# First attention of a two-layer kernel: split values stationary, probabilities moving in 256 columns

## What is computed

```
q = rmsnorm(zq, q_norm_g); k = rmsnorm(zk, k_norm_g); v = zv
y_a = dilated_attention(q, k, v)
y = concat([rmsnorm(y_c, g_out_conv), rmsnorm(y_a, g_out_attn)])
x = x + y @ w_out
```

## Time and profile before

| | us |
|---|---|
| median of three runs | 2596.24 (2596.04 to 2597.03) |
| the profiled execution's own time | 2594.65 |
| its span, first to last instruction | 2593.0 |
| PE busy in the span | 2542.1 (98%) |
| DVE, ACT, POOL busy | 1296.6, 1043.0, 1265.1 |
| mean granted TensorE clock | 0.995 of full speed |

### The profile page before, as it was taken

The page is one execution under the profiler, slowest core; times in us unless marked ns, Lnnn a source line. Parts: engine busy times, 40 slices in busy tenths (PEclk is TensorE's granted clock), DMA queues, the critical chain, the costliest instruction groups (busy, mean ns, idle before and its releaser), DMA issues.

```text
span 2593.0 us, 35106 instructions
## 1 busy us (share of the span) xinstructions
PE 2542.1 (98%) x12506; PEld 2121.9 (82%) x12506; DVE 1296.6 (50%) x2500; ACT 1043.0 (40%) x1955; POOL 1265.1 (49%) x940
## 2 busy tenths in 40 slices
PE   7999999999999999999999999989999999999999
PEld 6888888887888888888877777779888888888887
DVE  5314446178666663225367888677237333333222
ACT  6345553253333332214256666486234333232120
POOL 2122224457666665444525554364256666656441
PEclk9999999999999999999999999999999999999999
DMA  4242312412222235220323122220322222226311
GB/s 156 73 118 90 95 54 76 159 58 98 82 90 82 90 130 203 82 65 16 110 77 98 59 68 70 95 82 21 147 82 73 82 75 89 82 99 225 111 47 71
DMA packets 90205, 238.47 MB, mean 92 GB/s; under 512 B 10256, under 2 KB 23856, under 8 KB 89776
## 3 DMA queue, kind: packets, MB, share of 16 engines
q1 hardware_dynamic: 90032, 236.21, 26.8%
HBM read 180.60 MB, written 51.38 MB: 89 GB/s over the span
## 4 chain that ended last, share of the span: by engine, by line
PE 68%; DVE 3%; ACT 2%; issue 1%; POOL 1%; DMA 1%; SPq 0%; ACTq 0%; DVEq 0%; POOLq 0%
PE PS L943 9%; PE PS L944 9%; PE PS L945 9%; PE PS L961 6%; PE PS L963 6%; PE PS L962 6%; PE PS L690 5%; PE PS L692 4%; PE PS L691 4%; PE PS L1213 2%; PE PS L1193 1%; DVE YT L2086 1%; PE PS L913 1%; PE PS L1178 1%; PE PS L1179 1%
## 5 line engine op out<-in xcount | busy, mean ns | idle before, releaser
L690 PE MATMUL PS<-Hh,Wl 128*128 128x512 f32 x1072 | 438.3, 409 | 12.3 <-DVE Hl L1344 9.7
L692 PE MATMUL PS<-Hh,Wh 128*128 128x512 f32 x1072 | 421.0, 393 | 0.0
L691 PE MATMUL PS<-Hl,Wh 128*128 128x512 f32 x1072 | 419.8, 392 | 0.0
L3135 POOL TENSOR_TENSOR Wl<-Wr,Wh 128x512 fp32r<-128x512 f32 (+1 forms) x158 | 210.1, 1352 | 341.6 <-ACT Wh L2270 341.4
L3239 POOL TENSOR_TENSOR RG<-RW,RG 128x512 fp32r<-128x512 f32 x176 | 246.4, 1404 | 134.0 <-ACT RG L2546 133.8
L1757 DVE TENSOR_TENSOR XA<-PS,XA 128x512 f32<-128x512 f32 x192 | 132.5, 691 | 331.4 <-PE PS L963 331.4
L961 PE MATMUL PS<-Hh,RG 128*128 128x512 f32 x704 | 274.1, 389 | 0.5 <-issue 0.4
L963 PE MATMUL PS<-Hh,RG 128*128 128x512 f32 x704 | 273.9, 389 | 0.0
L962 PE MATMUL PS<-Hl,RG 128*128 128x512 f32 x704 | 273.9, 389 | 0.0
L3239 POOL TENSOR_TENSOR RG<-SW,RG 128x512 fp32r<-128x512 f32 x120 | 164.7, 1373 | 175.3 <-ACT RG L2546 150.0
L943 PE MATMUL PS<-Hh,RG 128*128 128x512 f32 x640 | 249.0, 389 | 0.0
(11 more groups left out here) (356 smaller groups left out, 5136.1 us busy)
## 6 DMA issues: line engine op xcount, KB each, us to landing
RW<-in_wg SPq DMA_DIRECT2D x44, 512.0 KB, 3.6
RW<-in_wu SPq DMA_DIRECT2D x44, 512.0 KB, 4.5
R<-in_wd SPq DMA_DIRECT2D x88, 256.0 KB, 3.0
hgscr<-GB SPq DMA_DIRECT2D x44, 512.0 KB, 2.6
G<-hgscr SPq DMA_DIRECT2D x40, 512.0 KB, 6.8
Wr<-in_wi SPq DMA_DIRECT2D x27, 512.0 KB, 3.4
Wr<-in_wo SPq DMA_DIRECT2D x16, 512.0 KB, 3.4
spill<-X SPq DMA_DIRECT2D x16, 512.0 KB, 2.6
```

Source lines behind the costliest of these rows:

```text
L690: pe.matmul(ps(b), k.Wl[:, s, wc], xh[:, kx, sl], start=kk == 0, stop=False)
L691: pe.matmul(ps(b), k.Wh[:, s, wc], xl[:, kx, sl], start=False, stop=False)
L692: i = pe.matmul(ps(b), k.Wh[:, s, wc], xh[:, kx, sl], start=False, stop=kk == nk - 1)
L3135: i = pool.tensor_tensor(k.Wl[:, s, c], k.Wr[:, s, c], k.Wh[:, s, c].bitcast(F32), ALU.subtract)
```

## The change

Values: each of the 8 position blocks is evicted twice, by ACT as the f32r high part and by DVE as the low part (value minus high part), into staging buffers `VS`. SP sends them out: head 0 straight to its place `V2[0]` (64 KB per block, rows of 512 bytes), the other heads (448 KB per block, rows of 512 bytes) to a scratch tensor in HBM, and waits for all of these before its weave goes on. `V2[h % 2]` holds for one head and each key block 128 columns: 64 of the head's high parts, 64 of its low parts (swapped for odd heads); `values_load` fetches the next head in tick i = 2.

Output: `V2` is the stationary operand and the transposed probabilities move, in 256 columns: the high part of 128 queries, then the low part. Bank 3 then holds, by features, high x high, high x low and (in the other 64 partitions) low x high. ACT copies the last (`att_c`), DVE adds the first two (a reduction), POOL adds the copy four ticks after the step's own tick. `sums_row` spreads the reciprocals of four blocks over the rows by four transposes on PE (16 times in all), and DVE multiplies half a head by them.

Probabilities: ACT copies all n blocks of the transposed probabilities as their high part, DVE subtracts that from PSUM for the low part and only this frees banks 6 and 7.

Norm: the outputs already lie by features. `attention1_norm` squares four tiles of 128x1024 on ACT, DVE adds them up, PE sums over features in 8 one-column matmuls, ACT takes the root, PE spreads it in 8 transposes, DVE applies it with the gain. 32 transposes, 32 scalings and 32 squares of 128x128 go.

```
--- attention1, tensor
-                if i > 3 and k.wide(1, r) is not None:
-                    pe.wait_ge(*at("att_ptv", 1, k.wide(1, r)))
+                if i == 4 and h:
+                    pe.wait_ge(*at("y_own", h - 1, 1))
...
-                for c in range(i + 1):
-                    m = pe.matmul(ps(3, 128), k.PT[:, r % 2, 128 * c:128 * c + 128],
-                                  k.Vt[:, c, 128 * (h // 2):128 * (h // 2) + 128], start=c == 0, stop=c == i)
+                pe.wait_ge(*at("att_lo", 1, r))
+                for c in range(i + 1):
+                    m = pe.matmul(ps(3, 256), k.V2[h % 2][:, c, :], k.PT[r % 2][:, c, :], start=c == 0, stop=c == i)
                 m.then_inc(*up(("full", 3), "att_o", 1, r))
+            for h, half in k.row_due(s):
+                sums_row(h, half)
--- attention1, vector
-                if i > 3:
-                    w = 128 * (i + 1) - 512
-                    dve.wait_ge(*at("att_t", 1, r))
-                    dve.tensor_copy(k.PT[:, r % 2, 512:512 + w], ps(7, w)).then_inc(*up("att_ptv", "att_ptv", 1, r))
+                dve.wait_ge(*at("att_t", 1, r))
+                dve.wait_ge(*at("att_pt", 1, r))
+                dve.tensor_tensor(k.PT[r % 2][:, 0:i + 1, 128:256],
+                                  k.PS[:, 512 * 6:512 * 6 + W].rearrange("p (c n) -> p c n", c=i + 1),
+                                  k.PT[r % 2][:, 0:i + 1, 0:128].bitcast(F32), ALU.subtract).then_inc(
+                    *up(("free", 6), "att_lo", 1, r))
...
-                dve.tensor_scalar(out, k.PS[:, o:o + 64], k.rx[:, r:r + 1], None, ALU.mult).then_inc(
-                    *up(("free", 3), "att_y", 1, r))
+                dve.wait_ge(*at("att_c", 1, r))
+                dve.tensor_reduce(k.ya(h)[own, 128 * i:128 * i + 128],
+                                  k.PS[own, 512 * 3:512 * 3 + 256].rearrange("p (z q) -> p q z", z=2),
+                                  mybir.AxisListType.X, ALU.add).then_inc(*up(("free", 3), "att_y", 1, r))
+            for h, half in k.row_due(s, 1):
+                sums_row(h, half)
--- attention1, scalar
-                act.activation(PT[:, r % 2, 0:w], ps(6, w), ACT.Copy).then_inc(*up(("free", 6), "att_pt", a, r))
+                act.activation(k.PT[r % 2][:, 0:i + 1, 0:128],
+                               k.PS[:, 512 * 6:512 * 6 + W].rearrange("p (c n) -> p c n", c=i + 1), ACT.Copy).then_inc(
+                    *up("att_pt", "att_pt", 1, r))
+            if 3 <= s < n + 3:
+                r = s - 3
+                own, other = k.sides(ATT1[r][0])
+                act.wait_ge(*at("att_o", 1, r))
+                if r >= 2:
+                    act.wait_ge(*at("y_add", r - 2))
+                act.activation(k.sml[own, 256 + 128 * (r % 2):384 + 128 * (r % 2)], k.PS[other, 512 * 3:512 * 3 + 128],
+                               ACT.Copy).then_inc(*up("yn_a", "att_c", 1, r))
--- attention1, gpsimd
+            if s >= 4:
+                r = s - 4
...
+                pool.wait_ge(*at("att_c", 1, r))
+                pool.wait_ge(*at("att_y", 1, r))
...
+                pool.tensor_tensor(y, y, k.sml[own, 256 + 128 * (r % 2):384 + 128 * (r % 2)], ALU.add).then_inc(
+                    *up("rot_g", "y_add", r))
--- sync
+    for i in range(8):
+        v = k.VS[i][:, :, :, :].bitcast(F32).rearrange("p h z n -> p (h z n)")
+        sp.wait_ge(*at("vt", i))
+        sp.dma_start(k.V2[0][:, i, :].bitcast(F32), v[:, 0:128]).then_inc(*up(("d_s", i), "v2_in", 0, i))
+        sp.dma_start(k.vs.rearrange("h p n -> p h n")[:, 1:8, 128 * i:128 * i + 128],
+                     v[:, 128:1024].rearrange("p (h n) -> p h n", h=7)).then_inc(*up(("d_y", i), "v_kept", i))
+    for i in range(8):
+        sp.wait_ge(*at("v_kept", i))
     bg.add(tables1())
```

More of the change, by code:

```diff
@@ L484, in ya, with sides, row_due @@
         return k.YX[:, :] if h < 2 else k.QT[:, h // 2 - 1, :]
+    def sides(h):
+        own = slice(64 * (h % 2), 64 * (h % 2) + 64)
+        return own, slice(64 - 64 * (h % 2), 128 - 64 * (h % 2))
+    def row_due(s, late=0):
+        return [(h, half) for h in range(8) for half in range(2) if s == 8 * h + 10 + 2 * half + late]
+    k.sides, k.row_due = sides, row_due
     def eps_at(half):
@@ L781, in tensor, with sums_row @@
                 qk_slot(between[i])
+    def sums_row(h, half):
+        r = 8 * h + 4 * half
+        take(7)
+        pe.wait_ge(*at("att_rec", 1, r + 3))
+        for i in range(4):
+            m = pe.transpose(ps(7)[:, 128 * i:128 * i + 128], k.rx[:, r + i:r + i + 1].to_broadcast([128, 128]), ident)
+        m.then_inc(*up(("full", 7), "y_row", h, half))
     def attention1():
         n = len(ATT1)
-        for s in range(n + 3):
+        for s in range(n + 6):
             if 2 <= s <= n + 1:
@@ L1392, in vector, with sums_row @@
         qk_slot(t)
+    for i in range(8):
+        dve.wait_ge(*at("v", i))
+        dve.wait_ge(*at("vt_hi", i))
+        dve.scalar_tensor_tensor(out=k.VS[i][:, :, 1, :], in0=ps(i).rearrange("p (h n) -> p h n", h=8),
+                                 scalar=k.sml[:, 112 + i:113 + i], in1=k.VS[i][:, :, 0, :].bitcast(F32), op0=ALU.mult,
+                                 op1=ALU.subtract).then_inc(*up(("free", i), "vt", i))
+    def sums_row(h, half):
+        own, _ = k.sides(h)
+        y = k.ya(h)[own, half_of(half)]
+        dve.wait_ge(*at("y_row", h, half))
+        dve.wait_ge(*at("y_add", 8 * h + 3 + 4 * half))
+        dve.tensor_tensor(y, y, k.PS[own, 512 * 7:512 * 8], ALU.mult).then_inc(*up(("free", 7), "y_own", h, half))
     def attention1():
         n = len(ATT1)
-        for s in range(n + 3):
+        for s in range(n + 6):
             if 2 <= s <= n + 1:
@@ L1450, in attention1_turn @@
+        for c in range(1, 4):
+            dve.wait_ge(*at("y_sq", 0))
+            dve.wait_ge(*at("y_sq", c))
+            if c > 1:
+                dve.wait_ge(*at("y_sum", c - 1))
+            dve.tensor_tensor(k.PP[:, 2, :], k.PP[:, 2, :], k.PP[:, (c + 1) % 2, :], ALU.add).then_inc(*up("yn_v", "y_sum", c))
             yield
+        for _ in range(4):
             yield
+        dve.wait_ge(*at("y_std"))
+        dve.reciprocal(k.sml[:, 80:88], k.sml[:, 88:96]).then_inc(*up("yn_v", "y_root"))
@@ new lines, in attention1_norm @@
+        for _ in range(2):
+            yield
+        for half in range(2):
+            sl = half_of(half)
+            dve.wait_ge(*at("y_spread", half))
+            for c in range(4):
+                i = dve.scalar_tensor_tensor(out=k.KT[:, c, sl], in0=k.ya(2 * c)[:, sl], scalar=col("g_out_attn", c),
+                                             in1=ps(6 + half), op0=ALU.mult, op1=ALU.mult)
+                if c == 3:
+                    i.then_inc(*up(("free", 6 + half), "yk", half))
+                yield
@@ L3555, in tables1 @@
                 key_load(h + 1)
+            if i == 2 and h < 7:
+                sp.wait_ge(*at("att_o", 1, 8 * h - 1) if h else at("v_kept", 6))
+                values_load(h + 1)
             if i == 4 and h < 7:
```

202 lines of the change are left out of this document (113 added, 89 removed).

## The result

| | before | after |
|---|---|---|
| median of the runs | 2596.14 us (2595.13 to 2597.03) | **2637.02 us** (2634.62 to 2639.22) |
| profiled execution, its span | 2594.65, 2593.0 | 2636.77, 2635.5 |
| first to last exponential of the attention | 169.94 to 368.41 = 198.5 | 169.41 to 408.37 = **239.0** |

(PE is TensorE, PEld its weight loads, DVE VectorE, ACT ScalarE, POOL GpSimd, SP the engine that issues the loads and stores. Tile i stands for a head's step with i + 1 key blocks; "the interval 4 to 5" is the time from the start of the exponential of tile 4 to that of tile 5.)

The account below looks back on a forecast made before the run. The prediction took a closed ACT-DVE chain (copy, subtract, maximum, exponential) to bound the changed attention: +18.5 us there, +1 ahead, -2.5 behind, sum +17, so 2613 us. Range 2598 to 2636 us.

Parts of the forecast that it names:

- The sign: Whole kernel: the change makes it slower, chance 0.83, against 0.10 for the same and 0.07 for faster.
- One closed chain over two engines: Attention ticks: none can be shorter than copy + subtract + maximum + exp on ACT and DVE; attention 217 us against 198.5.
- Start, "+1, between 0 and 6": Ahead of the attention: storing values by 16 DMAs, with SP waiting for all, costs +1 us, between 0 and 6.
- The table of eight intervals: Attention: each tick's interval from chain, ACT extras and PE's round, together 26.4 us per head; PE alone would need 22.6.
- PE 1.07 ahead: Attention tick 2: PE runs 1.07 us ahead, so the interval is 2.36 us although PE's round is 3.43.
- DVE's 64-partition reduction and the 16 row products lie beside exp: nothing.: Attention: these added DVE operations run beside ACT's exponential and cost nothing.
- Query loads, 3 of 0 to 8: Attention: ACT's waits for query loads, 8.0 us before, add 3 us, anywhere from 0 to 8.
- PE -27 us: PE's own work: cheaper output matmuls, less added row transposes and with a shorter final part, make it fall by 27 us.
- Behind, -2.5: After the attention: the last three output groups and the shorter final part, less one row group, save 2.5 us.
- Rival 3: Attention: PE's idling lowers the granted clock; once per head adds 16 us, 2629 us; chance 0.07.
- Rival 4: Attention: loads drive the chain, ACT waits of 4 us in every head add 8 x 3, 2635 us; chance 0.05.
- Rival 1: Attention: PE still sets the pace and loses 27 us of work, 2569 us; chance 0.05.

Follow-up runs that it names:

- rows early: Changed kernel with the second row product of a head and the transposes before it one tick earlier, and the first product too: 2636.82 us, ratio 1.0146.
- the last one: Changed kernel plus all three edits of order and place, head 1's keys and queries fetched earlier, query split at tile 2, two-part bank hand-over: 2592.57 us, ratio 0.9983.

## Why the prediction failed

The sign, which had a chance of 0.83, and the mechanism were right: a closed chain over ACT and DVE made the attention longer though PE had less to do. The size was not: 41 us against 17, and 1 us outside the range. Of the 22 us by which the attention overran its forecast (239.0 against 217), the trace of the changed kernel gives 7.3 to the load of head 1's keys, which the sum did not have, some 5 to two ticks of the table (an estimate from heads 3 and 4, times seven) and at most some 4 to the wait for the row product (what the profile of rows early lost). The rest, 5 us or more, stays open. By the prediction's own steps:

- *"One closed chain over two engines" sets the tick.* Right: 57 and 60 of 64 waits; an added microsecond of subtraction costs about one; opened, the chain gives 29 us back. The durations were as worked out: copies of 1024 and 896 columns took 1.026 and 0.908 us (1.02 and 0.91 were drawn on from 512), the subtraction of 1024 took 1.22. The Trainium skill's estimate for the copy of 1024 columns (ScalarE: Activation LUTs, What ACT_TABLE_LOAD costs) was 1039 ns; the trace is 13 ns under it.
- *Start, "+1, between 0 and 6".* The step that failed most: 7.3 us (the interval 4 to 5 of head 0, 11.29, less the chain's 4.0), and inside the attention, not ahead of it. The first copies were looked at, and not the load of head 1's keys, which SP issues behind its wait for all the stores and which ACT's next copy stands behind. SP's queue was named in the text, its next customer was not. Issuing it earlier did not mend it by itself, since the DMA engines are full there.
- *The table of eight intervals.* Heads 3 and 4, in which ACT waits for no load, took 29.2 and 29.3 us, where the table has 26.4 and the forecast 27 to 28 with what was added. Ticks 0 and 1 came out (6.5 us from head 3 to head 4, against 6.63), in part by luck: the table has a query split in tick 1, but the program runs each split behind the exponential of its tick, so it lands one tick later, and in its place ACT stood 0.45 us for the eight transposes. The misplaced splits hardly move the sum. Ticks 2 and 3 failed: 4.71 in the table, 5.4 and 5.5 measured (intervals 1 to 2 and 2 to 3, and 0.2 since the table counts from end to end). *"PE 1.07 ahead"* was the term: PE needs the subtraction of eight blocks before it can send the next transpose, which starts only 0.3 us ahead of the exponential of tile 1 (266.42), its round then takes 3.55 us, and ACT's copy waits for its end:

```profile
266.10 0.33 PE L819 MATMUL PS<-mats,PP 128*128 128x128 f32 x1
...
269.65 0.38 PE L819 MATMUL PS<-mats,PP 128*128 128x128 f32 x2
```

```profile
270.07 0.39 ACT L2517 ACTIVATE PT<-PS 128x256 fp32r<-128x256 f32 x1 [0.61 <-PE PS L819]
```

- *"DVE's 64-partition reduction and the 16 row products lie beside exp: nothing."* The step failed as a wait: not their 0.69 us, but that PE's transposes of tile 4 wait for the second product of the head before (17.5 us, 7 times), and behind the longest of these waits run at the lower clock. The interval 5 to 6, where the chain with its query split gives 4.1, took 4.56 to 5.25 us in heads 1 to 7; in head 3 that is the weight split, which ACT had to take there too. With the wait removed the attention was 3.9 us shorter in one profile and the whole was not, so what it was worth stays open.
- *Query loads, 3 of 0 to 8.* One of 3.58 us made the interval 1 to 2 of head 5 6.01 us, where the others have 2.2 to 3.3: right in size.
- *PE -27 us.* It was 15 to 16, which cost nothing here but decides what the change could ever bring. Output matmuls are 0.12 us apart, as taken, but where PE runs without standing the 0.08 us behind each group stayed (five take 0.68 us, six 0.80, seven 0.92), and the spread rows cost 9.7, not 7.7.
- *Behind, -2.5.* From the last exponential to the end the profiles have 2224.6 us before, 2227.1 after and 2224.8 to 2233.8 in the variants. None shows the gain; the runs of one kernel spread over several microseconds, so how much was lost in its place isn't told apart.

Rival 3 (the clock) was given 0.07 and by itself 2629. Its sign, a clock below 1.00, came together with the forecast: the granted clock was 0.94 over the stretch, since late loads and the wait for the product made standstills of 3 us and more. What it cost is not shown by itself; the same 12274 matmuls are busy for 2541.7 us in the changed kernel and for 2526.8 in the last one, an estimate of 15 us for PE's own work, not all of it on the path. Rival 4 (loads drive the chain) had 2635 us; by its own numbers, 2613 + 24, it is 2637, the time measured, and that is chance: ACT stood 4.2 us for queries in all, in two places. The rivals were priced one at a time, and the time was what several give together. That narrowed the range at its upper end.

Rival 1 (PE sets the pace) would be 2569 us. The Trainium skill's rule (Perfetto Trace Analysis, Identifying the Most-Contended Engine) is to optimize the engine with the highest occupancy first, which stands on that rival's side. Here the busiest engine did get less to do, and the kernel got slower.

## What to carry to other kernels

Before taking work from the busiest engine, write down for each bank and each in-order queue what must happen between one use and the next, around all engines: the longest such loop set the tick here, whatever the busy shares said. The order of two independent instructions on one engine can be worth more than the work that a change saves (29 us against 16), and such orders are to be tried together on all engines: one half of this move alone cost 17 us, the other alone gave 14. When a transfer is late, look at what the DMA engines carry and at the next transfer in the same queue before moving one of them.

## Unexpected about the hardware

- The stores of split values with rows of 512 bytes keep the DMA engines full: while eight of 448 KB and eight of 64 KB go out, the DMA share is about 1 from 162 to 178 us, at 274 to 345 GB/s, and a 256 KB load issued 3 us earlier into that was in use only 0.2 us earlier.
- Consecutive VectorE subtractions of 128 columns, 0.28 us each by their records, overlap: 288 of them are busy for 62.6 us together, 0.22 each.
- TensorE stood from 180.3 to 188.0 us; its granted clock was 0.98 from 180.3 to 184 and 0.50 from 184 to 190, its lower level. Behind a standstill of 3.29 us a score matmul of 512 columns took 0.78 us, and 0.48 five microseconds on.
